# A 128-token share of an expert layer gathered row by row and summed on VectorE; the other 384 tokens stay dense and are summed token-major in PSUM

## The reference, cut to what matters

```python
q = (h @ w_q).reshape(bsz, s, PK_HEADS, PK_DIM)          # 8 heads
...
v1, i1 = lax.top_k(s1, PK_TOPK); v2, i2 = lax.top_k(s2, PK_TOPK)
best, c = lax.top_k(cand, PK_TOPK)                        # 16 of 256
expert = e1 * N_KEYS + e2                                 # of 16384
gate = jax.nn.softmax(best, axis=-1)
...
u_sel = jnp.take(u_tab, et, axis=0)
act = gelu(einsum('tkd,td->tk', u_sel, xt))
v_sel = jnp.take(v_tab, et, axis=0)
out = einsum('tk,tkd->td', gt * act, v_sel)
```

## Time and profile before

| stage (from the span's start) | us | what runs |
|---|---|---|
| 0 to 620 | 620 | up to the top-k; not touched except for one dropped column of `vec` |
| 620 to 798 | 178 | 32 score blocks beside top-k |
| 798 to 1088.6 | 290.6 | weights, with 32 score blocks |
| 1088.6 to 1110.0 | 21.4 | the change-over to the value stage |
| 1110.0 to 2143.9 | 1033.9 | values, 32 groups |
| 2143.9 to 2164.0 | 20.1 | end |
| profiled span | 2164.0 | |
| median of the runs | 2167.5 | 3.5 over the span |

### The profile page before, as it was taken

One profiled execution on the slowest core, in us unless ns is written; L12 is line 12 of the kernel. 1 busy time (PEld: TensorE's weight loads), 2 busy tenths in 40 slices (PEclk: granted clock), 3 DMA queues, 4 the chain that ended last, 5 costly groups with the idle time before them and its releaser, 6 DMA issues.

```text
span 2164.0 us, 37156 instructions
## 1 busy us (share of the span) xinstructions
PE 2091.6 (97%) x12954; PEld 1744.5 (81%) x12954; DVE 1367.4 (63%) x2823; ACT 839.8 (39%) x1185; POOL 371.4 (17%) x462
## 2 busy tenths in 40 slices
PE   5999999997999999999989999999999999999997
PEld 3878888785878888888868888888888888888885
DVE  5478676557999977777745555555554554554555
ACT  4555343433222246666633333332333333332332
POOL 0000000100035469999800000000000000000000
PEclk9999999998999999999999999999999999999998
DMA  4211111432234445555564344344344444444431
GB/s 147 87 50 51 65 56 60 175 127 78 69 107 146 144 164 204 202 202 201 202 219 155 121 160 154 122 156 152 128 155 146 135 155 143 135 159 135 141 102 39
DMA packets 156781, 289.47 MB, mean 134 GB/s; under 512 B 10496, under 2 KB 76160, under 8 KB 154144
## 3 DMA queue, kind: packets, MB, share of 16 engines
q1 hardware_dynamic: 153856, 276.86, 38.4%
q0 software_dynamic: 2848, 11.54, 1.5%
HBM read 231.73 MB, written 56.62 MB: 133 GB/s over the span
## 4 chain that ended last, share of the span: by engine, by line
PE 70%; issue 9%; DVE 1%; DMA 1%; POOL 0%; ACT 0%; DVEq 0%; SPq 0%; POOLq 0%; ACTq 0%
PE unit L350 70%; DMA gl<-g_dram 0%; POOL uL L2033 0%; DMA g_dram<-ge 0%; DVE x L1997 0%; DMA sgw<-gate_dram 0%; DVE rs L1994 0%; DVE rs L1433 0%; DVE x L1942 0%; DVE aL L1932 0%; DVE af L1927 0%; PE unit L789 0%; DVE mb L1789 0%; ACT aH L966 0%; DVE wL L1424 0%
## 5 line engine op out<-in xcount | busy, mean ns | idle before, releaser
L350 PE MATMUL unit<-h2H,uH 128*128 128x512 f32 x1024 | 410.4, 401 | 2.9 <-POOL uL L2033 2.9
L350 PE MATMUL unit<-aH,vH 128*128 128x512 f32 x1024 | 399.4, 390 | 10.5 <-DVE vL L1936 10.5
L350 PE MATMUL unit<-h2L,uH 128*128 128x512 f32 x1024 | 399.2, 390 | 0.0
L350 PE MATMUL unit<-aL,vH 128*128 128x512 f32 x1024 | 399.1, 390 | 0.0
L350 PE MATMUL unit<-aH,vL 128*128 128x512 f32 x1024 | 399.1, 390 | 0.0
L350 PE MATMUL unit<-h2H,uL 128*128 128x512 f32 x1024 | 398.9, 390 | 0.0
L1936 DVE TENSOR_TENSOR vL<-vraw,vH 128x512 fp32r<-128x512 f32 x256 | 176.3, 690 | 235.9 <-ACT vH L966 235.9
L966 ACT ACTIVATE vH<-vraw 128x512 fp32r<-128x512 f32 x256 | 161.1, 630 | 414.6 <-PE unit L350 414.6
L2050 POOL TENSOR_SCALAR oh<-cst,e2s 128x128 f32<-128x128 f32 x384 | 264.9, 707 | 20.2 <-PE unit L350 15.4
L350 PEld LDWEIGHTS unit<-aH,vH 128*128 128x128 f32 x1024 | 192.7, 188 | 51.1 <-DVE vL L1936 10.9
L350 PEld LDWEIGHTS unit<-h2H,uH 128*128 128x128 f32 x1024 | 192.8, 188 | 40.6 <-POOL uL L2033 5.1
(11 more groups left out here) (274 smaller groups left out, 2971.2 us busy)
## 6 DMA issues: line engine op xcount, KB each, us to landing
uraw<-uT SPq DMA_DIRECT2D x128, 512.0 KB, 4.3
vraw<-v_tab SPq DMA_DIRECT2D x256, 256.0 KB, 2.8
wraw<-wall SPq DMA_DIRECT2D x68, 512.0 KB, 3.7
w_dram<-wst SPq DMA_DIRECT2D x16, 2048.0 KB, 6.6
wg<-w_dram SPq DMA_DIRECT2D x32, 1024.0 KB, 6.5
g_dram<-ge SPq DMA_DIRECT2D x64, 256.0 KB, 2.2
gl<-g_dram SPq DMA_DIRECT2D x32, 512.0 KB, 7.5
gate_dram<-gst POOLq DMA_DIRECT2D x16, 256.0 KB, 2.4
```

What stands on the lines that cost most here:

```text
L350: return pe.matmul(out, lhsT, rhs, start=start, stop=stop, skip_group_check=True)
```

## The change

Tokens 384 to 511 (tile `DT` = 3) leave the dense path. TD = 384 tokens stay in it.

- **Dense path.** Score matmuls, gelus, `weigh`, `a_high` and `a_low` take 384 columns in place of 512. The weight stage has 96 batches (WI = 6 rounds of 16) in place of 128, and 24 score blocks beside them (PRE_W); the other PRE_T = 40 of the 64 blocks that are done ahead stand beside the top-k.
- **Values token-major.** The activations of 128 tokens are now the stationary operand and v the moving one, 512 columns wide. Three token tiles of 1024 channels take six of the eight banks and stay there over all 32 groups, begun with `x1` itself by 24 transposing matmuls. `add_up` is gone. There is one sweep; a v block is now loaded and split as one 128 x 1024 piece in place of two of 512.
- **Half of `v_low` on POOL.** Blocks 1 and 3 of each group (POOL_V).
- **Sparse path.** For token tile 3 the expert of each token and slot is `idx` (L1926). POOL fetches 128 rows for each slot by indirect DMA, one row for each partition (token), into a ring of 8 buffers of 4 KB. A group pair takes 8 slots: in the even group DVE forms 8 dot products with `h2T` (`dot`), ACT a small gelu, and in the odd group DVE multiplies by the gate and adds 8 v rows to `accs` (`add_row`). That is 256 fetches, 128 dots and 128 additions. `h2T` and `accs` come from 24 small matmuls before the scores.
- **End.** Squares with a row sum on ACT, four scalings of 128 x 1024 on DVE, four stores of 512 KB.

The core of the diff:

```diff
-NTB = T // T_W
+DT = TT - 1
+TD = DT * P
+NTB = TD // T_W
+WI = TD // (2 * T_W)
 NPRE = PRE * NG
+PRE_W = 4 * WI
+PRE_T = NPRE - PRE_W
+SR = 8
+POOL_V = (1, 3)
...
+            for t in range(DT):
+                for c in range(DC):
+                    last = mm(acc[t][:, c // 4, (c % 4) * P:(c % 4 + 1) * P], x1[:, c, tile(t)], C(C_ID),
+                              c % 4 == 0, False)
...
-                    last = mm3(bank[j][:, :], vH[:, u % 4, j * P:(j + 1) * P], vL[:, u % 4, j * P:(j + 1) * P],
-                               aH[:, slot, :], aL[:, slot, :], g == 0, g == G - 1)
...
+                for t in range(DT):
+                    for l, r in ((aH, vH), (aH, vL), (aL, vH)):
+                        for k in range(2):
+                            last = mm(acc[t][:, k, :], l[:, g, tile(t)], r[:, g, k * 512:(k + 1) * 512], False, final)
...
+            def group(q, more):
+                for g in range(G):
+                    unit(q, g, not more and g == G - 1)
+                    if more and g % 2:
+                        scores(NPRE + 2 * (q + 1) + g // 2, g // 2)
...
+            stt(idx[:, :], ee[:, DT, 0, :], float(NK), ee[:, DT, 1, :], ALU.mult, ALU.add).then_inc(idx_ready, 1)
...
+            def dot(i, k):
+
+                dve.wait_ge(row_loaded[k], 32 * i + 16)
+                stt(ring[k][:, :], ring[k][:, :], 1.0, h2T[:, :], ALU.mult, ALU.mult,
+                    accum_out=spd[:, k:k + 1]).then_inc(row_used, 1)
...
+            def add_row(i, k):
+
+                dve.wait_ge(row_loaded[k], 32 * i + 32)
+                if k == 0:
+                    dve.wait_ge(sp_gated, i + 1)
+                dve.wait_ge(row_used, 2 * SR * i + SR + k)
+                stt(accs[:, :], ring[k][:, :], spa[:, k:k + 1], accs[:, :], ALU.mult, ALU.add).then_inc(row_used, 1)
...
+            def fetch(n):
+
+                i, half, k = n // (2 * SR), n // SR % 2, n % SR
+                if n >= SR:
+                    pool.wait_ge(row_used, n - SR + 1)
+                pool.indirect_dma_start(
+                    out=ring[k][:, :], out_offset=None, in_=(u_tab, v_tab)[half],
+                    in_offset=bass.IndirectOffsetOnAxis(ap=idx[:, SR * i + k:SR * i + k + 1], axis=0)
+                ).then_inc(row_loaded[k], 16)
+
+            def v_low(q, g):
+                pool.wait_ge(vh_ready, G * q + g + 1)
+                pool.tensor_tensor(vL[:, g, :], vraw[:, g, :], vH[:, g, :], ALU.subtract).then_inc(vl_pool, 1)
```

More of the change, by code:

```diff
@@ L288, in build @@
         u_loaded = [sem(f"u{i}_loaded") for i in range(G)]
-        v_loaded = [sem(f"v{i}_loaded") for i in range(2 * G)]
+        v_loaded = [sem(f"v{i}_loaded") for i in range(G)]
         wg_loaded = [sem(f"wg{i}_loaded") for i in range(2)]
@@ L1261, in _ @@
                 split_h(W_Q + m + 2)
+            for name, dst in (("ht", h2T), ("xs", accs)):
+                for k in range(2):
+                    wait_filled(act, f"{name}{k}")
+                    fn(dst[:, k * 512:(k + 1) * 512], ps(f"{name}{k}")[:, :], ACT.Copy).then_inc(
+                        take_sem(f"{name}{k}"), 1)
             def u_high(n, lap, slot):
@@ L1957, in step, with row @@
                 base = 2 * (1 - par)
-                weigh(q, i, par, G - 1)
+                def row(k):
+                    if par == 0:
+                        dot(i, k)
+                    else:
+                        add_row(i, k)
+                weigh(i, par, 0)
+                v_low(q, 0)
+                a_low(q, 0)
+                if not par:
+                    row(0)
+                weigh(i, par, 1)
+                if not par:
+                    row(1)
+                v_low(q, 1)
+                a_low(q, 1)
+                if par:
+                    gate(i)
+                    row(0)
+                    row(1)
+                row(2)
+                weigh(i, par, 2)
+                row(3)
+                a_low(q, 2)
                 if more:
                     u_low(NPRE + 2 * (q + 1), base)
-                a_low(q, par, G - 1)
-                for u in (4, 5, 6):
-                    v_low(q, u)
-                add_up(q, 0)
-                v_low(q, 7)
-                if not more:
-                    for c in range(4):
-                        grow_sum(2, rs3, sq3, c)
-                if more:
-                    nq, nlap, npar = q + 1, i + par, 1 - par
-                    weigh(nq, nlap, npar, 0)
-                    weigh(nq, nlap, npar, 1)
-                    a_low(nq, npar, 0)
-                    a_low(nq, npar, 1)
-                    u_low(NPRE + 2 * nq + 1, base + 1)
-                    weigh(nq, nlap, npar, 2)
-                    a_low(nq, npar, 2)
-                    for u in (0, 1, 2):
-                        v_low(nq, u)
-                add_up(q, 1)
-                if more:
-                    v_low(nq, 3)
+                row(4)
+                v_low(q, 2)
+                row(5)
+                weigh(i, par, 3)
+                row(6)
+                a_low(q, 3)
+                if more:
+                    u_low(NPRE + 2 * (q + 1) + 1, base + 1)
+                v_low(q, 3)
+                row(7)
             with dve.Fori(0, NG // 2 - 1) as i:
@@ L2053, in _, with v_low @@
                 pool.wait_ge(oh2_ready, 16 * i + 16)
+            def fetch(n):
[6 more added lines that the diff above has]
+                ).then_inc(row_loaded[k], 16)
+            def v_low(q, g):
+                pool.wait_ge(vh_ready, G * q + g + 1)
+                pool.tensor_tensor(vL[:, g, :], vraw[:, g, :], vH[:, g, :], ALU.subtract).then_inc(vl_pool, 1)
+            pool.wait_ge(idx_ready, 1)
+            pool.wait_ge(acc_begun, 1)
+            for i in range(2):
+                pool.wait_ge(wst_stored[i], 16 * NTB // 2)
+            for n in range(SR):
+                fetch(n)
+            for q in range(NG):
+                for part in range(2):
+                    if 2 * part + 1 in POOL_V:
+                        v_low(q, 2 * part + 1)
+                    if q + 1 < NG:
+                        for k in range(SR // 2):
+                            fetch(SR * (q + 1) + SR // 2 * part + k)
 def constants():
```

346 lines of the change are left out of this document (183 added, 163 removed).

## The result

The changed kernel takes 1828.17 us (median of 4 runs, 1826.83 to 1830.72), the kernel before 2168.16 us on the same chip. The ratio is 0.8436, 95% interval 0.8423 to 0.8449: 340 us less. The profiled execution's span is 1826.9 us. The forecast was 1880 us, and 1820 us by the first rival.

What follows compares the result with a forecast made beforehand. PE was taken to bound the weight and value stages before, POOL and DVE after. Terms 620 + 179 + 204 + 24 + 842 + 8 = 1877 us of span, so 1880 us; range 1812 to 1995.

Steps and rivals of the forecast that it cites:

- the first rival: Value stage: PE stays the bound, fetches cost DVE next to nothing; stage 782 us, total 1820 us; chance 0.25.
- The forecast's own case: Value stage: DVE becomes the bound, groups between 25.3 and 28.9 us, 26.4 booked; chance 0.50.
- Weight stage: Weight stage: POOL becomes the bound at 33.9 us a round; six rounds 204 us, where PE alone needs 187.
- Matmuls: Score matmuls: 384 columns take 0.174 us each, against 0.227 for 512; weight loads should hide.
- Stage beside the top-k: 620 to 798 us: no gain, DVE's top-k not shortened; 7 us given to POOL hold-ups by DVE; 179 us booked.
- Value stage, the step that failed: Value stage: eight fetches shut DVE out for 1.9 us a group, making DVE the bound at 26.4 us.
- 19.7 + 4.8 = 24.5 us: Value stage, one group: DVE's own work 19.7 us plus 4.8 for POOL's two `v_low`, level with PE's 24.7.
- Transfers: Value stage: 8.52 MB a group takes 23.2 to 26.3 us, level with PE and DVE, taken as hidden.
- What the prediction drew from it: Value stage: by the skill page, DVE's two-input operations leave descriptor writing alone; only the fetches' index reads could collide.

Runs made afterwards that it cites:

- Both split experiments: POOL builds two of four one-hot matrices instead of three, DVE two: against the changed kernel, 1812.87 us; same edit in the kernel before, 2166.98 us.
- pe_light: Changed kernel without the product `aL x vH`, 24 of each group's 120 matmuls; loads, splits, fetches and row operations stay: 1824.59 us.
- the port: Kernel without `aL x vH`, all `v_low` moved from POOL to DVE, against the same kernel with half on POOL: 1782.32 us.
- the order: Kernel without `aL x vH`, all `v_low` on DVE: DVE's list reordered to fill waits, ACT's small gelu ahead of its copies: 1732.12 us.
- the split: Kernel without `aL x vH`, `v_low` on DVE, lists reordered: one-hot work also divided two and two between POOL and DVE: 1713.97 us.

## Why the prediction was right in its number's range and wrong in its likeliest case

The sign and most of the size came as forecast, but the measured 1828 us lie in the range of 1812 to 1995 only because it reached down to the first rival, which had a chance of 0.25. The forecast's own case, groups of 25.3 to 28.9 us, did not come.

- **Weight stage: right.** 204 us booked by POOL's batch, 205.4 measured; POOL's 288 comparisons take 714 ns each, where the earlier trace rows has 707. Both split experiments, with and without gain, confirm that the bound passed from PE to POOL.
- **Matmuls: right.** 384 columns start 0.173 us apart for 0.174, and the group measures 24.69 us for PE's 24.7.
- **Stage beside the top-k: the size was off, 185.5 for 179.** The working gave the round of ACT and POOL a slack of 0.7 us. It left out the gelu of 0.49 that stands in it, and took 2.40 us for a subtraction that takes 2.80 on average beside DVE. The slack is below zero. The 7 us booked for hold-ups by DVE were too few: at 4.48 us in place of 4.17, 38 blocks are 12 us late, and PE transposes the results at 796.2 us, not 790. That the reordered ACT list brought nothing speaks for the exclusion as the stronger part.
- **Value stage, the step that failed:** "I take the smallest operation of POOL that reads SBUF, the copy of 0.237 us, since a fetch must read its 128 indices: 1.9 us for eight. DVE then needs 26.4 us for a group and is the bound." The 1.9 us are 0: no operation of DVE is longer beside a fetch. With all fetches and no POOL subtraction, the longest dot is 1.225 us; with no fetches and POOL's subtractions, DVE's busy time is unchanged (566.8 for 567.4 us). The first rival's group of 24.7 us came. Its 1820 us are 8 below the measured time: 6.5 us beside the top-k, 1.4 in the weight stage and 7.5 in the value stage (789.5 for 782) are more, 4.1 in the change-over and 1.4 at the end less, and the profiled span stands 1.3 under the median in place of 3.5.
- **"19.7 + 4.8 = 24.5 us" came out right by two errors that cancel.** The recorded lengths overlap: DVE's 1.22 us operations start 1.14 us apart, its 0.55 us ones 0.47. By starts, eight of 0.47, four of 1.14, eight row operations of 1.14 or 1.19 and half a gate are 17.7 us for the booked 19.7. The exclusion is 1.83 for a `v_low` in place of 2.4, 3.7 a group. And 3.1 us are waits inside the list that the sum did not have (700 - 611.23 us idle in 28.35 groups). Nearly all are these three, from 1040 to 1800 us:

```profile
DVE vL L1985 <- ACT vH L1010: 50.0, 31, 1.6
DVE spa L1995 <- ACT spg L1010: 29.9, 16, 1.9
...
DVE aL L1979 <- ACT aH L1010: 10.6, 16, 0.7
```

Together that is 24.5 us again; the light kernel shows 24.65.
- **The rival was right in its number and only half right in its reason.** "PE stays the bound" holds to within 0.04 us a group: DVE's list is as long as PE's. Without `pe_light` the profile, with PE at 700.00 of 700 us, would have hidden that. The page of the changed kernel gives one hint, the shares of the span in the chain that ended last:

```profile
issue 23%; DVE 18%; PE 17%; POOL 13%; ACT 3%; DMA 1%; POOLq 0%; DVEq 0%; ACTq 0%; SPq 0%
```

In the value stage this chain has PE in one piece for eleven groups, to 1348.2 us, and from there on leaves it in every group, mostly for DVE's operations. A stage with slack behind PE does not show that: the earlier trace rows has 1033.89 us of PE in one piece, and the kernel without the row path 784.60. First the changed kernel, then that one:

```profile
1075.39 272.81 PE unit L381 x1320
```
```profile
1032.40 784.60 PE unit L381 x3780
```
- **Transfers: right to be hidden, wrong to be level.** Value groups at 342 GB/s do not wait, and the same traffic goes at 393 GB/s when the engines are quicker. The smallest rate in the earlier trace rows, 286 GB/s over 2 us, was no limit for the value stage.

The Trainium skill, page "SBUF — State Buffer", section "SBUF: two separate sides", was weighed before the result. Its rule that an operation with two SBUF inputs and a GpSimd operation that reads SBUF exclude each other is shown here, with 1.83 us on average for each `v_low`. That descriptor writing is starved by VectorE's 2-port modes no run here shows. What the prediction drew from it, that two-input operations would leave the writing alone, holds in one direction only: DVE loses nothing, the fetch grows from 0.94 to 1.75 or 1.97 us. Whether its index read or its writing waits is open.

The 340 us by the measured stages: 244.4 from the values, 85.2 from the weights, 1.5 from the change-over and 13.5 from the end, less 7.5 beside the top-k: 337.1 of span. The medians differ by 340.0, and the profiled executions stand 4.2 and 1.3 us under them.

**The better versions.** Without leaving anything out, the kernel with the one-hot work split takes 1812.87 us. Without the product `aL x vH` the best takes 1713.97. The steps from 1824.6 are the port (42 us), the order (50 us) and the split (18 us). The first two were run with the light matmuls only. With PE's full 24.7 us a group there should be no room for them: leaving out the whole row path gave 2 us.

## What to carry to other kernels

An engine that is busy 100% of a stage does not say how far the next one is behind. Take a fifth of its work away, and the time tells: here 3.6 us of 170 came, because another engine's list, waits and exclusions counted, was as long to within 0.04 us a group. A sum of busy times needs two corrections before it is set against such a bound: starts in place of recorded lengths, and the waits inside an in-order list. And a GpSimd subtraction beside VectorE's two-input operations is paid by VectorE: here 1.8 to 2.3 us for each, where doing it itself costs VectorE 1.14. The better place for such work may be VectorE.

## What was not expected of the hardware

- An indirect fetch of 128 rows of 4 KB costs GpSimd 0.93 to 2.02 us and a gap of 0.30, and costs VectorE nothing, even beside operations with two SBUF inputs. DVE never waits for a row in the changed kernel.
- The transfers of a value group, rows from random places among them, went at 393 GB/s over 600 us.
- The exclusion costs VectorE 2.20 us where its queue is full, on average 1.83, and 2.3 with two behind each other, for each GpSimd subtraction that takes 2.40 alone: GpSimd waits up to 1 us for VectorE's running operation (3.41 recorded), then VectorE waits for it.
